# A bf16 copy of the projection weights in DRAM, for an eight-core decoder trunk on Trainium2

## What is computed

```python
mod = silu(c) @ w_ada + b_ada                  # 1024 x 6144
h = rmsnorm(x, norm1_g) * (1 + sc1) + sh1
proj = h @ w_in                                # 1024 x 4608
b_a, c_a, h_a, v_b, g_b, mg_a, mg_b = split(proj)
y_a = (b_a * causal_dwconv3(c_a * h_a)) @ w_out_a          # 512 x 1024
conv_b = causal_dwconv31(v_b * sigmoid(g_b)) + bias
y_b = silu(layernorm(conv_b)) @ w_out_b                    # 512 x 1024
x = x + gt1 * ((sigmoid(mg_a) * y_a + sigmoid(mg_b) * y_b) @ w_o)   # 1024 x 1024
h2 = rmsnorm(x, norm2_g) * (1 + sc2) + sh2
x = x + gt2 * moe(h2)                          # 16 experts, top 2 of one group
y = rmsnorm(x, final_norm_g)
```

## Time and profile before

| | |
|---|---|
| median of 3 runs | 1710.7 us (1708.82 to 1711.91) |
| the profiled execution | 1712.47 us |
| its span on the slowest core (core 4) | 1710.9 us |
| spans of the eight cores | 1683.9 to 1710.9 us |
| TensorE busy | 1376.6 us (80%) |
| VectorE, ScalarE, GpSimd busy | 775.3, 449.6, 174.7 us |
| bytes moved by GpSimd's DMA queue | 105.92 MB in 187552 packets |
| read from HBM, written to HBM | 221.85 MB, 9.76 MB |
| first part of the program | 0 to about 761 us |

### The profile page before, as it was taken

One profiled execution on the slowest core, in us unless ns is written; L12 is line 12 of the kernel. 1 busy time (PEld: TensorE's weight loads), 2 busy tenths in 40 slices (PEclk: granted clock), 3 DMA queues, 4 the chain that ended last, 5 costly groups with the idle time before them and its releaser, 6 DMA issues.

```text
span 1710.9 us, 23373 instructions; the slowest of 8 cores (1683.9 to 1710.9 us)
## 1 busy us (share of the span) xinstructions
PE 1376.6 (80%) x7465; PEld 682.1 (40%) x7508; DVE 775.3 (45%) x1847; ACT 449.6 (26%) x845; POOL 174.7 (10%) x214
## 2 busy tenths in 40 slices
PE   0488798798798668755776799998999999999994
PEld 0244344343344334531333445444454544445441
DVE  0105244352541633455455355455545545555565
ACT  1336225414522521624333111110111110111132
POOL 2121120221121112020000010100101010000000
PEclk9999899999999989976999899999999999999997
DMA  9995998899599299739000050220505040040013
GB/s 165 141 141 87 140 141 127 104 145 152 67 149 148 28 157 142 103 45 129 1 1 1 1 75 1 42 34 1 74 1 75 1 60 16 2 73 1 1 71 132
DMA packets 200549, 127.22 MB, mean 74 GB/s; under 512 B 4848, under 2 KB 194032, under 8 KB 200432
## 3 DMA queue, kind: packets, MB, share of 16 engines
q0 software_dynamic: 187552, 105.92, 50.8%
q1 hardware_dynamic: 12880, 19.81, 3.6%
HBM read 221.85 MB, written 9.76 MB: 135 GB/s over the span
## 4 chain that ended last, share of the span: by engine, by line
PE 53%; DMA 20%; DVE 11%; issue 8%; ACT 6%; DVEq 1%; POOL 0%; ACTq 0%; POOLq 0%; SPq 0%
PE ps_all L935 13%; DMA ring<-w_in 13%; PE ps_all L938 13%; PE ps_all L962 8%; PE ps_all L466 6%; PE ps_all L590 5%; DVE xT_sb L969 4%; DMA ring<-w_out_b 4%; DMA ring<-w_ada 3%; PE ps_all L843 2%; PE ps_all L930 1%; DVE tlb L944 1%; ACT dgb L537 1%; ACT h2T L802 1%; PE ps_all L656 1%
## 5 line engine op out<-in xcount | busy, mean ns | idle before, releaser
L466 PE MATMUL ps_all<-hT,ring 128*128 128x448 bf16 (+1 forms) x1440 | 279.5, 352 | 79.4 <-DMA ring<-w_in 65.6
L962 PE MATMUL ps_all<-sqB,wC 128*128 128x384 bf16 (+2 forms) x1271 | 266.8, 350 | 76.7 <-DVE xT_sb L969 55.3
L935 PE MATMUL ps_all<-h2T,wA 128*128 128x384 bf16 (+2 forms) x1250 | 255.4, 344 | 7.0 <-ACT slb L942 4.5
L938 PE MATMUL ps_all<-h2T,wB 128*128 128x512 bf16 (+2 forms) x1278 | 256.0, 343 | 1.7 <-DVE tlb L944 1.6
L942 ACT ACTIVATE slb<-ps_all 128x512 f32<-128x512 f32 (+2 forms) x160 | 83.1, 522 | 613.0 <-PE ps_all L935 534.0
L969 DVE SCALAR_TENSOR_TENSOR xT_sb<-ps_all,modT,xT_sb 128x512 f32<-128x512 f32 (+2 forms) x320 | 202.4, 641 | 62.3 <-PE ps_all L962 55.7
L466 PEld LDWEIGHTS ps_all<-hT,ring 128*128 128x128 bf16 x1440 | 140.0, 100 | 217.5 <-issue 113.2
L944 DVE TENSOR_TENSOR tlb<-ps_all,slb 128x512 f32<-128x512 f32 (+2 forms) x160 | 95.7, 598 | 278.3 <-PE ps_all L938 272.6
L962 PEld LDWEIGHTS ps_all<-sqB,wC 128*128 128x128 bf16 x1280 | 113.6, 99 | 223.9 <-issue 155.8
L938 PEld LDWEIGHTS ps_all<-h2T,wB 128*128 128x128 bf16 x1280 | 125.7, 98 | 106.6 <-issue 4.5
L935 PEld LDWEIGHTS ps_all<-h2T,wA 128*128 128x128 bf16 x1280 | 119.3, 98 | 112.0 <-issue 20.5
(11 more groups left out here) (146 smaller groups left out, 1017.1 us busy)
## 6 DMA issues: line engine op xcount, KB each, us to landing
ring<-w_in POOLq DMA_DIRECT2D x90, 512.0 KB, 16.8
ring<-w_ada POOLq DMA_DIRECT2D x24, 512.0 KB, 19.9
ring<-w_o POOLq DMA_DIRECT2D x20, 512.0 KB, 13.3
wA<-w POOLq DMA_DIRECT2D x16, 512.0 KB, 11.4
wB<-w POOLq DMA_DIRECT2D x16, 512.0 KB, 13.2
wC<-w POOLq DMA_DIRECT2D x16, 512.0 KB, 14.8
xT_sb<-xT SPq DMA_DIRECT2D x4, 1792.0 KB, 12.9
ring<-w_out_a POOLq DMA_DIRECT2D x10, 512.0 KB, 14.6
```

The lines of the kernel that those rows point to most:

```text
L466: return [e.matmul(PS(bank, n), wv[:, kc, j * 128:(j + 1) * 128], hT[:, kc, 0:n], start=(kc == 0), stop=(kc == NDC - 1)) for kc in range(NDC)]
L935: S.add(PE, lambda e, el=el, f=f, hb=hb: [e.matmul(PS(hb, n), wA[slot][:, el, kc, f * 128:(f + 1) * 128], h2T[:, kc, st.t0:st.t0 + n], sta ...
L938: S.add(PE, lambda e, el=el, f=f, hb=hb: [e.matmul(PS(hb + 1, n), wB[slot][:, el, kc, f * 128:(f + 1) * 128], h2T[:, kc, st.t0:st.t0 + n], ...
L962: out.append(e.matmul(PS(yb, n), wC[slot][:, el, f, m * 128:(m + 1) * 128], ab[:, el * 2 + f, 0:n], start=(i == 0), stop=(i == 3)))
```

## The change

A DRAM tensor `wcache` of 26 blocks of 128 x 2048 bf16 is added. In pass 0 (`tag == 0`) a block is loaded and cast as before. When its slot is about to be loaded again, a DMA on GpSimd's queue first stores the slot's content to `wcache`. In passes 1 to 4 the block is loaded from `wcache`, bf16 to bf16, 4096 contiguous bytes for each partition. `w_ada` is loaded as before.

```diff
+    NWC = 26
+    wc_d = nc.dram_tensor("wcache", [NWC, 128, 2048], BF16).ap()
...
-        def ring_load(src_ap, shape3, name):
+        slot_pending = {}
+
+        def ring_load(src_ap, shape3, name, store_as=None):
             slot = ring_state["n"] % NRING
             ring_state["n"] += 1
             a_, b_ = shape3
             assert a_ * b_ == 2048
+            if slot in slot_pending:
+                bid = slot_pending.pop(slot)
+                S.add(POOL, lambda e, bid=bid, slot=slot: [e.dma_start(out=wc_d[bid], in_=ring[slot][:, :])],
+                      reads=[("ring", slot)], writes=[("wc", bid)], dma=("wcst", slot), ndma=1, name="wc_store")
             view = ring[slot][:, 0:a_ * b_].rearrange("p (a b) -> p a b", a=a_)
-            S.add(POOL, lambda e, o=view, i=src_ap: [e.dma_start(out=o, in_=i)],
-                  writes=[("ring", slot)], dma=("ring", slot), ndma=1, name=name)
+            if src_ap is None:
+                S.add(POOL, lambda e, slot=slot, bid=store_as: [e.dma_start(out=ring[slot][:, :], in_=wc_d[bid])],
+                      reads=[("wc", store_as)], writes=[("ring", slot)], dma=("ring", slot), ndma=1, name=name)
+            else:
+                S.add(POOL, lambda e, o=view, i=src_ap: [e.dma_start(out=o, in_=i)],
+                      writes=[("ring", slot)], dma=("ring", slot), ndma=1, name=name)
+                if store_as is not None:
+                    slot_pending[slot] = store_as
             return slot, view
...
+                    if tag == 0:
+                        if kind == "w_in":
+                            src = w_in_v[:, :, idx * 256:(idx + 1) * 256]
...
+                        wcache[key] = ring_load(src, shape, kind, store_as=bid)
+                    else:
+                        wcache[key] = ring_load(None, shape, kind + "_c", store_as=bid)
```

More of the change, by code:

```diff
@@ L337, in ring_load @@
             assert a_ * b_ == 2048
+            if slot in slot_pending:
+                bid = slot_pending.pop(slot)
+                S.add(POOL, lambda e, bid=bid, slot=slot: [e.dma_start(out=wc_d[bid], in_=ring[slot][:, :])],
+                      reads=[("ring", slot)], writes=[("wc", bid)], dma=("wcst", slot), ndma=1, name="wc_store")
             view = ring[slot][:, 0:a_ * b_].rearrange("p (a b) -> p a b", a=a_)
-            S.add(POOL, lambda e, o=view, i=src_ap: [e.dma_start(out=o, in_=i)],
-                  writes=[("ring", slot)], dma=("ring", slot), ndma=1, name=name)
+            if src_ap is None:
[6 more added lines that the diff above has]
+                    slot_pending[slot] = store_as
             return slot, view
         wcache = {}
+        WC_BASE = {"w_in": 0, "w_o": 18, "w_oa": 22, "w_ob": 24}
         def wblk(kind, tag, idx):
@@ L347, in wblk @@
             if key not in wcache:
[L348 to L356, removed]
-                    wcache[key] = ring_load(w_ada_v[:, :, idx * 256:(idx + 1) * 256], (NDC, 256), "w_ada")
+                if kind == "w_ada":
+                    wcache[key] = ring_load(w_ada_v[:, :, idx * 256:(idx + 1) * 256], (NDC, 256), "w_ada")
+                else:
+                    bid = WC_BASE[kind] + idx
+                    shape = (4, 512) if kind in ("w_oa", "w_ob") else (NDC, 256)
+                    if tag == 0:
+                        if kind == "w_in":
+                            src = w_in_v[:, :, idx * 256:(idx + 1) * 256]
+                        elif kind == "w_o":
+                            src = w_o_v[:, :, idx * 256:(idx + 1) * 256]
+                        elif kind == "w_oa":
+                            src = w_oa_v[:, :, idx * 512:(idx + 1) * 512]
+                        else:
+                            src = w_ob_v[:, :, idx * 512:(idx + 1) * 512]
+                        wcache[key] = ring_load(src, shape, kind, store_as=bid)
+                    else:
+                        wcache[key] = ring_load(None, shape, kind + "_c", store_as=bid)
             return wcache[key]
```

## The result

| | before | after |
|---|---|---|
| median of ten runs | 1711.96 us | 1759.73 us |
| the profiled execution | 1712.47 us | 1751.89 us |
| slowest core, its span | core 4, 1710.9 us | core 6, 1750.1 us |
| spans of the eight cores | 1683.9 to 1710.9 us | 1740.7 to 1750.1 us |

The change makes the kernel slower: ratio 1.0245, interval 1.0213 to 1.0277, where 1704 us had been forecast.

The account below looks back on a forecast made before the run. The prediction took the kernel as bound by TensorE, with stretches starving for weights. Pass 0 +41.9, clock +3, pass 1 0, passes 2 to 4 -12, -12, -28 gave -7.1 us: 1704 us, range 1684 to 1730.

Parts of the forecast that it names:

- The round trip: Pass 0: each block costs T, one load plus one store plus semaphores, 7.6 us, ends 6.0 and 9.7 us.
- The load, 6.0 us: Pass 0: a load from issue to landing on an idle queue, leaning to the lower of 8.1, 6.7 and 5.5 us.
- The store, 1.5 us: Pass 0: only the store's data adds, 524 KB at about 360 GB/s; its whole latency would be 3.2 us.
- The semaphore, 0.1 us: Pass 0: the term for semaphores in each block's T, 0.1 us.
- the prediction's own formula: Pass 0: first store done at 79.6, then 11 trips of 7.6 us, last load and matmuls, ending at 172.2; cost 41.9 us.
- 3 us for the clock: Pass 0: 3 us added for the last block at half speed, since TensorE stands idle more than half the time.
- the round trip is longer, and the change ends slower: Pass 0 rival: the store's whole 3.2 us adds to a 6.2 us load, T = 9.4, 1729 us; chance 0.22.
- Pass 1, counted at nothing with 6 us either way: Pass 1: ten more stores, nearly covered; `w_o` loads start some 6 us earlier and `out_proj` ends where before; 0 us.
- Passes 2 to 4: Lose their DMA wait, limited by ScalarE's eviction behind the layer norm and by the mixer: -12, -12 and -28 us.
- the store hides: Pass 0 rival: the store runs beside the load, T = 6.0, pass 0 costs 25.8 with the clock, 1685 us; chance 0.14.
- the clock keeps the later passes low: Passes 2 to 4 rival: TensorE's pauses keep its clock low, each pass loses up to 3.4 us, 1714 us; chance 0.12.
- reloads no faster: Passes 2 to 4 rival: loads from `wcache` are no faster, so 52 us are missing, 1756 us; chance 0.02.

Follow-up runs that it names:

- the chain without stores: The kernel before, with pass 0's `w_in` loads from the seventh on and four `w_ada` loads each waiting for the landing of the load ahead: 1742.07 us.
- quarter store: The change with float32 weights loaded and cast in passes 1 to 4 as before, each store writing 512 of 2048 columns: 1771.12 us in its one run.
- the kernel with one store: The change with only one block stored and every reload reading it, so weights in passes 1 to 4 are wrong: 1656.11 us, ratio 0.9678.

## Why the prediction was wrong

It forecast 1704 us, and 1752 us were measured in the profiled execution, beyond the range's 1730. The mechanism, one load and one store under way at a time, was right. Its price was wrong in pass 0, by the round trip, and in pass 1, which was counted at nothing.

**The round trip, the step that failed first.** The prediction had T = 6.0 + 1.5 + 0.1 = 7.6 us; measured are 9.35 (core 6) and 9.47 (core 4, 80.73 to 184.91 in eleven). Term by term:

- The load, 6.0 us: right for a load by itself, 5.7 in the chain without stores. With a full store issued behind it the load lands at 7.2. These 1.2 us are the largest part of the miss: the prediction had the time of a load with nothing behind it, and no term for what the store does to it.
- The store, 1.5 us: right. It comes behind the load, as the prediction took it, and lands 1.3 us after it.
- The semaphore, 0.1 us: measured 0.6 to 0.7 from a landing to the next issue. Over eleven trips that is 6 us. The rows before held nothing that would show it, and the prediction gave the term without a reason.

The changed kernel's landings and its DMA rate on core 4 from 100 to 160 us (40 equal slices):

```profile
GB/s 14 0 41 127 172 351 8 0 41 121 162 358 22 0 44 130 156 355 14 0 54 113 197 323 11 0 35 124 166 355 19 11 33 117 154 351 23 22 0 20
...
ring<-w_in POOLq DMA_DIRECT2D x7, 512.0 KB, 7.2
wcache<-ring POOLq DMA_DIRECT2D x7, 512.0 KB, 7.6
```

One period is about six slices of 1.5 us: one or two with nothing, one at 40 GB/s, two at 110 to 200, one at over 350. The last is the store's rate of the earlier trace rows. The load lands at 7.2 us, the store at 0.9 + 7.6 = 8.5, and 0.6 us later the next load goes out: 9.1, the usual trip. Two of the eleven trips took 11 us, which makes the means 9.35 and 9.47.

The packets of the trace can be told apart by size, 512 bytes for a casting load and 4096 for a store. On core 4, in the median of the trips from 85 to 180 us, the load's packets run from 1.7 to 6.9 us after its issue and the store's from 6.0 to 8.2. In the chain without stores the load's run from 1.6 to 5.4. So the load's data take 1.4 us longer, although the packets of its own store begin only in the last of these microseconds. What slows them is not shown. It grows with the store's bytes (5.6 us for the load's last packet with a quarter store), and stores of other cores at the same time are a rival that no kernel here tests.

With the measured sizes the prediction's own formula closes: 11 x (9.35 - 7.6) = 19.3 us, the first store 1.1 us later (80.66 for 79.6), the last load 1.3 us longer, and the last sixteen matmuls 1.8 us longer give 172.2 + 23.5 = 195.7 us; measured are 195.5 on core 6. These are measured sizes put into the formula, so they don't test it anew, but they leave nothing over: pass 0 had no other fault. Of the 3 us for the clock those 1.8 us are what came; at the lower clock the other matmuls mostly hide under the wait for the next block.

**The rival "the round trip is longer, and the change ends slower"** is what happened, with the threshold that it named: from T = 8.2 on. Its T of 9.4 was nearly exact, by luck, and its 1729 us still lay 23 us too low, for the most part by pass 1 and the core, below. It had a chance of 0.22 because the prediction took "only its data adds" over "its whole latency adds". The truth was neither, as the quarter store shows: the store adds its data, and makes the load ahead of it slower by nearly as much. The Trainium skill, "DMA: Bandwidth & Descriptors" (section on the anatomy of one DMA), prices each DMA at about 2.0 us and its bytes over 436e3, and an estimate from it gives the same 3.2 us for the store as the 9.4 has. This case's runs agree with its total and not with the fixed part adding to the trip: with it a store of 128 KB would still cost 2.3 us, an estimate from that page, and the quarter stores added 0.6.

**Pass 1, counted at nothing with 6 us either way**, cost 16 us on core 4 and 22 on core 6. The prediction checked the right places and put T = 7.6 into each. On core 4 the first `w_o` load was to go out 6 us earlier in the pass and went out 0.7 us earlier, since it waits for a store too, and the three gaps behind it are 8.7 us instead of 7.6. The fourth comes some 8.8 us later than forecast. At that pace each load takes far longer than the 3.2 us of matmuls it feeds. TensorE on core 6:

```profile
306.37 5.05 PE L695 MATMUL ps_all<-merged,ring 128*128 128x448 bf16 x16 [5.84 <-DMA ring<-w_o]
```

It also took the gates' pairs to keep the old pace, and they didn't (the three waits above). The kernel that caches `w_in` alone puts 24 us on these stores. Of the passes' gain from reloads, pass 1 would have had 12 us (the kernel with one store), of which the prediction counted 6, as `w_o` loads that move earlier; the stores cost these too.

**Passes 2 to 4: right.** -12, -12 and -28 us were forecast, and -12.3, -12.6 and -26.2 measured on core 4. The saved waits ran into the two limits named. TensorE on core 6 at the start of pass 2:

```profile
394.56 3.19 PE L489 MATMUL ps_all<-hT,ring 128*128 128x448 bf16 x16 [0.91 <-DMA ring<-wcache]
403.58 2.77 PE L489 MATMUL ps_all<-hT,ring 128*128 128x448 bf16 x7 [5.83 <-ACT ca L499]
```

and the ScalarE instruction that it waits for:

```profile
402.85 0.59 ACT L499 ACTIVATE ca<-ps_all 128x448 f32<-128x448 f32 x1
```

Two chunks early, then 5.83 us for the eviction behind the layer norm: idle time with another name, as forecast. The rivals "the store hides", "the clock keeps the later passes low" and "reloads no faster" all fall.

**The core, a step that wasn't there.** The whole sum was made on core 4, the slowest of the profiled execution. In each execution of the kernel before whose cores are on record and that the comparisons use, one core of each pair (0 and 1, 2 and 3, 4 and 5, 6 and 7) lies ahead of the other, by 8 to 26 us, and which one it is changes from one execution to the next. With the change that is gone: the pairs of the profiled execution differ by 1 to 9 us. No run here shows what the two of a pair share. In the profiled execution before, core 6 was one of those ahead. It waited 35.6 us for `w_in` from 170 to 760 us in the trace before, core 4 63.2, and its span was 1687.4 us. It had less to win (30 us in passes 2 to 4 against 51) and paid the same toll: 69 us in pass 0, 22 in pass 1. So it went from 23 us ahead to 7 behind core 4 and became the metric. At the forecast price the two would have met at some 1703 us, so this step decided nothing there. The 7 us are this execution's: in the changed kernel's others the slowest core lay 0 to 9 us behind core 4.

## What to carry to other kernels

A ring hides latency only as deep as the number of transfers that may be under way; a write-back placed directly ahead of the load that takes its slot makes a ring of six a ring of one, at one whole load and store for each block. Issue the write-back when the block has landed, with one or two other loads between it and the load that takes its slot: here that is worth 77 us for the same bytes. A transfer that comes behind another can make the one ahead slower, so take the price of a pair from a pair. When a change adds the same cost to every core and a gain that differs between cores, work the sum for the core that gains least as well as for the slowest.

## What the runs showed of the hardware

- A 512 KB store issued 0.9 us behind a 512 KB casting load lands 1.3 us after that load and makes it land at 7.2 instead of 5.7 us. What the store adds grows with its bytes: round trips of 6.4, 7.0 and 8.8 us with no store, one of 128 KB and one of 512 KB.
- From a landing to the issue that waits for it on GpSimd's queue 0.6 to 0.7 us pass.
- A bf16 block from `wcache` lands in 4.6 us (median of 104), a casting load on an idle queue in 5.7, and with the queue full the casting load moves 138 GB/s.
- In a stretch of which TensorE paused for 39%, in waits of up to 6.5 us, its mean granted clock was 0.76, between its levels of 0.5 and 1; before, with 9% of pauses in the stretch from 80 us to the gates, it was 1.00.
- With casting loads in every pass one core of each pair is 8 to 26 us ahead of the other, another one from execution to execution. In the changed kernel's profiled execution the pairs differ by 1 to 9 us.
